# One stage for sample attention and sample mixers, and five raw buffers between the projection passes

## What is computed

```python
h = RMSNorm(x) * (1 + scale1(c)) + shift1(c)
proj = h @ w_in                     # columns of the mixers A, B, C, D
A: softmax attention over the own chunk of 64 and the 8 chunks before, with a relative bias
B: mLSTM: num = inter * (q @ c_state) + wqk @ v;  c = decay * c + (ws k)^T v;  n likewise
C: Mamba-2 SSD: y = (cb * dec * dt) @ x + exp(cs) * (C @ h_state);  h = exp(cs_end) * h + (wl x)^T B
D: gMLP spatial gating over chunks of 128
x = x + gate1(c) * (concat(A, B, C, D) @ w_out)
h2 = RMSNorm(x) * (1 + scale2(c)) + shift2(c)
x = x + gate2(c) * ((silu(causal_dwconv3(h2 @ w_gate)) * (h2 @ w_up)) @ w_down)
```

## Time and profile before

| | us |
|---|---|
| median of 3 runs | 3292.2 |
| the runs | 3286.8 to 3297.0 |
| profiled execution | 3301.0 |
| its span | 3299.0 |
| modulation and start | 0 to 147.2 |
| token pass | 147.2 to 514.7 |
| between the passes | 514.7 to 536.7 |
| channel pass | 536.7 to 831 |
| change of stage | 831 to 853.7 |
| sample attention | 853.7 to 970.5 |
| sample mixers | 970.5 to 1084.4 |
| mixers | 1084.4 to 1653 |
| feed forward | 1653 to 3299 |

### The profile page before, as it was taken

The page is one execution under the profiler, slowest core; times in us unless marked ns, Lnnn a source line. Parts: engine busy times, 40 slices in busy tenths (PEclk is TensorE's granted clock), DMA queues, the critical chain, the costliest instruction groups (busy, mean ns, idle before and its releaser), DMA issues.

```text
span 3299.0 us, 41922 instructions
## 1 busy us (share of the span) xinstructions
PE 2921.4 (89%) x16186; PEld 2581.5 (78%) x16186; DVE 1330.0 (40%) x2523; ACT 986.1 (30%) x1680; POOL 236.7 (7%) x405
## 2 busy tenths in 40 slices
PE   4599997999366399999779999999999999999987
PEld 1388886999233278888679999879999978999975
DVE  2333324332125355545333333544333454544444
ACT  1133324332111135445322222432222333222333
POOL 0000000000000133333100000000000000000000
PEclk8699998999775699999889999999999999999998
DMA  9522214221511653433152222443222354322344
GB/s 301 189 90 90 99 63 136 86 78 60 130 35 10 190 162 119 141 126 118 61 131 64 64 64 85 151 154 111 67 64 63 105 162 122 116 76 70 95 129 141
DMA packets 338040, 356.26 MB, mean 108 GB/s; under 512 B 44295, under 2 KB 279435, under 8 KB 337460
## 3 DMA queue, kind: packets, MB, share of 16 engines
q1 hardware_dynamic: 329238, 352.34, 34.6%
q10 hardware_dynamic: 8672, 2.15, 0.4%
HBM read 286.56 MB, written 70.10 MB: 108 GB/s over the span
## 4 chain that ended last, share of the span: by engine, by line
PE 44%; DMA 2%; DVE 2%; SPq 1%; issue 1%; ACT 0%; POOL 0%; DVEq 0%
PE acc_ps L2734 13%; PE acc_ps L2690 10%; PE acc_ps L2691 10%; PE acc_ps L2692 10%; DMA w_raw<-in_f_w_down 1%; DVE w_lo L2879 0%; DMA xr<-scratch_x 0%; SPq L2640 0%; DVE y L2951 0%; ACT w_hi L2783 0%; DMA out_y_prompt<-y 0%; DVE xr L2945 0%; DMA ffn_gate_in<-scratch_ffn_gate 0%; DVE prod L2939 0%; DVE mid_lo L2929 0%
## 5 line engine op out<-in xcount | busy, mean ns | idle before, releaser
L2690 PE MATMUL acc_ps<-h_hi,w_hi 128*128 128x384 f32 (+1 forms) x2112 | 690.4, 327 | 7.2 <-DVE w_lo L2879 7.1
L2691 PE MATMUL acc_ps<-h_lo,w_hi 128*128 128x384 f32 (+1 forms) x2112 | 689.7, 327 | 0.0
L2692 PE MATMUL acc_ps<-h_hi,w_lo 128*128 128x384 f32 (+1 forms) x2112 | 689.6, 327 | 0.0
L2879 DVE TENSOR_TENSOR w_lo<-w_raw,w_hi 128x1024 fp32r<-128x1024 f32 x264 | 323.4, 1225 | 695.3 <-ACT w_hi L2783 684.7
L2783 ACT ACTIVATE w_hi<-w_raw 128x1024 fp32r<-128x1024 f32 x264 | 279.8, 1060 | 845.7 <-PE acc_ps L2692 524.2
L2690 PEld LDWEIGHTS acc_ps<-h_hi,w_hi 128*128 128x128 f32 x2112 | 398.0, 188 | 8.2 <-DVE w_lo L2879 7.5
L2691 PEld LDWEIGHTS acc_ps<-h_lo,w_hi 128*128 128x128 f32 x2112 | 398.0, 188 | 0.1
L2692 PEld LDWEIGHTS acc_ps<-h_hi,w_lo 128*128 128x128 f32 x2112 | 397.9, 188 | 0.0
L2734 PE MATMUL acc_ps<-w_hi,mid_hi 128*128 128x512 f32 x748 | 237.8, 400 | 33.0 <-DVE mid_lo L2929 32.9
L2734 PE MATMUL acc_ps<-w_hi,mid_lo 128*128 128x512 f32 x748 | 234.3, 395 | 0.0
L2734 PE MATMUL acc_ps<-w_lo,mid_hi 128*128 128x512 f32 x748 | 234.0, 394 | 0.0
(11 more groups left out here) (481 smaller groups left out, 4182.2 us busy)
## 6 DMA issues: line engine op xcount, KB each, us to landing
w_raw<-in_f_w_down SPq DMA_DIRECT2D x132, 512.0 KB, 3.5
w_raw<-in_f_w_gate SPq DMA_DIRECT2D x66, 512.0 KB, 3.9
w_raw<-in_f_w_up SPq DMA_DIRECT2D x66, 512.0 KB, 3.9
w_ada<-in_w_ada SPq DMA_DIRECT2D x12, 2048.0 KB
m_bc<-scratch_bc SPq DMA_DIRECT2D x16, 768.0 KB, 5.1
scratch_tok<-p_m SPq DMA_DIRECT2D x17, 640.0 KB, 2.9
m_tok<-scratch_tok SPq DMA_DIRECT2D x16, 640.0 KB, 4.7
scratch_ht<-p_m SPq DMA_DIRECT2D x17, 512.0 KB, 3.3
```

What stands on the lines that cost most here:

```text
L2690: t.matmul(dst, hi, h2_hi[:, k, cols], start=(k == 0), stop=False)
L2691: t.matmul(dst, hi, h2_lo[:, k, cols], start=False, stop=False)
L2692: last = t.matmul(dst, lo, h2_hi[:, k, cols], start=False, stop=(k == KD - 1))
L2879: v.tensor_tensor(w_lo[j][:], raw[j][:], w_hi[j][:], ALU.subtract).then_inc(s_lo[j], 1)
```

## The change

**Between the projection passes.** The raw buffers of the channel weights become five. Buffer 3 lies in `rows`, which the token pass uses for its input, buffer 4 in the last third of `ht_in`, which group 0 (two tiles of the three) leaves free; it is loaded in pieces of 128 columns. In the turn of the last tile, SP issues `load_w(3)`, `load_w(4)` and `load_ht(0)` ahead of `store_rows(15)`; pieces 5 to 15 wait for the piece five before. `spatial` of the last tile moves behind unit 1 of group 0.

**The sample stage.** `sample_attention` and `sample_mixers` become `sample_stage` (L1200 of the new file). Two streams share a tile of 128 rows (2 streams x 4 heads x 16 tokens), so there are four rounds. `q_blk` holds block-diagonal queries: 32 columns (two heads of one stream) against 128 rows. The scores of a round are four products 32x512 on four column groups of the array and four of 16 columns for the new keys; the output is ten products of 256 columns, alternating between two halves of the columns. The old states are read per stream: 32 products of 65x16 (`old_c`) and 32 of 64x16 (`old_h`), which are turned afterwards; the masks and folds go. Weighings and the decay of the states move from DVE to POOL. C's state is turned by 16 transposes of 128x128 and isn't turned back, since the decayed state is kept as it was loaded. SP's queue carries keys, values and C's state (24 loads; a partition's share of keys is 4 KB in one piece); 29 smaller loads stand on ACT's queue ahead of its first operation. SP stores in the order y, m, ya (two for a round), n and c of B, and C's state in eight.

**The last down pass.** It is written out without a loop and has four raw buffers: two more in free columns of `mid` (`raw_far`), in eight pieces of 128 columns. Load f waits for the low part of f - 4.

The core of the diff:

```diff
@@ projections
-                if m >= 3:
-                    sp.wait_ge(s_wlo, m - 2)
+                if m >= NRAW:
+                    sp.wait_ge(s_wlo, m - NRAW + 1)
+                elif m >= 3:
+                    sp.wait_ge(s_t, NTT)
...
+                if n == LASTN:
+                    load_w(3)
+                    load_w(4)
+                    load_ht(0)
                 if n >= 1:
                     store_rows(n - 1)
...
-            load_ht(0)
-            for m in range(3, 2 * KD):
+            for m in range(NRAW, 2 * KD):
                 load_w(m)
...
-                spatial(n)
...
                     chan_unit(g, u)
+                    if g == 0 and u == 1:
+                        spatial(LASTN)
@@ sample_stage, PE
+            def scores(j):
...
+                for b2 in range(2):
+                    for pair in range(2):
+                        b, at = 2 * j + b2, (2 * b2 + pair) * 32
+                        w = q_blk[:, b, pair].rearrange("p r t -> p (r t)")
+                        t.matmul(m[at:at + 32, B_S, :], w, k_t[:, pair, b, :], start=True, stop=True)
...
+            def attend(j):
...
+                for n in range(NPAST + 1):
+                    for b2 in range(2):
+                        b, rows = 2 * j + b2, slice(b2 * DH, (b2 + 1) * DH)
+                        if n < NPAST:
+                            t.matmul(o_ps[rows], prob_t[:, n, rows], v_in[:, b, n, :], start=(n == 0), stop=False)
+                        else:
+                            last = t.matmul(o_ps[rows], own_t[:, rows], v_new[:, b, :], start=False, stop=True)
...
+            def old_h():
...
+                for b in range(NB):
+                    for h in range(H):
+                        at = h // 2 * P + b * TS
+                        last = t.matmul(m[half(h), B_E, at:at + TS], hst[:, b // 2, h, b % 2 * DH:(b % 2 + 1) * DH],
+                                        xc[:, 4 + h // 2, b * TS:(b + 1) * TS], start=True, stop=True)
...
+            turn_k(0)
+            turn_k(1)
...
+            scores(0)
+            turn_ssm()
+            old_c()
+            turn_probs(0)
+            old_h()
+            turn_k(2)
+            turn_k(3)
+            attend(0)
+            turn_old()
+            scores(1)
+            rows_to_all()
+            turn_probs(1)
...
@@ sample_stage, DVE: a round's output
+                v.tensor_tensor(pick_o[:], o_ps.rearrange(heads, h=H), spread(head_inv[:], 2, DH), ALU.mult
+                                ).then_inc(E["out_masked"], 1)
+                dve.wait_ge(E["out_masked"], j + 1)
+                v.tensor_reduce(ya[:, j, :], pick_o[:].rearrange("p h d -> p d h"), AX, ALU.add).then_inc(E["ya_done"], 1)
@@ feed_forward
+        raw_far = [mid[:, 4 + KD * j:4 + KD * (j + 1), last_width:last_width + P] for j in range(2)]
...
+            def load_dn_last(f):
+                j, base = f % 2, down_unit(LAST, 1, 0)
+                sp.wait_ge(s_lo[j], base + max(0, f // 2 - 1))
+                if f % 4 < 2:
+                    sp.dma_start(raw[j][:], wd[f]).then_inc(s_raw[j], 16)
+                else:
+                    sp.dma_start(raw_far[j], wd[f].rearrange("p (k c) -> p k c", k=KD)).then_inc(s_far[j], 16)
```

More of the change, by code:

```diff
@@ L264, in projections @@
         raw = sb("raw", [P, 3 * XW])
-        w_raw = [raw[:, j * XW:(j + 1) * XW] for j in range(3)]
+        w_raw = [raw[:, j * XW:(j + 1) * XW].rearrange("p (n c) -> p n c", c=P) for j in range(3)]
+        w_raw += [rows[:, 3 * D:3 * D + XW].rearrange("p (n c) -> p n c", c=P), ht_in[:, 0:KX, 2 * P:TW]]
         ws_in = raw[:, 0:512].rearrange("p (g s) -> p g s", g=H)
@@ new lines, in new_c @@
+            def new_c():
+                for h in range(H):
+                    pe.wait_ge(E["vws_done"], h + 1)
+                    if h == 2:
+                        pe.wait_ge(E["dec_args"], 1)
+                    for q in range(2):
+                        last = t.matmul(m[half(h), (B_T, B_X)[h // 2] + q, 0:4 * W1], tok[:, T_KB + h * DH:T_KB + (h + 1) * DH],
+                                        vws[h % 2][:, 4 * q * W1:(4 * q + 4) * W1], start=True, stop=True)
+                    last.then_inc(E["c_ps"], 1)
@@ L1724, in mixers @@
+            add_c(2)
+            add_c(3)
+            extract(3)
+            for h in range(H):
+                add_h(h)
 def mixers(nc, sem, A, O, S, c, keep, par):
@@ L2657, in _ @@
                 for a in range(NPASS):
+                    if s == LAST and a == 1:
+                        for f in range(KF):
+                            load_dn_last(f)
+                            if f >= 3 and f - 3 < len(before(s, a)):
+                                store(before(s, a)[f - 3])
+                        continue
                     lo, hi = static_until(s, a)
@@ L2841, in _ @@
                 for a in range(NPASS):
+                    if s == LAST and a == 1:
+                        for f in range(KF):
+                            down_step_last(f)
+                            tile_part(f, before(s, a))
+                        continue
                     lo, hi = static_until(s, a)
```

801 lines of the change are left out of this document (437 added, 364 removed).

## The result

The changed kernel takes 3170.5 us as the median of four runs (3166.2 to 3176.7), the kernel before 3292.4 beside it. The ratio is 0.9622, with a 95% interval of 0.9604 to 0.9639: 124 us less by the ratio, 122 by the two medians. The forecast was 3179, in a range of 3153 to 3215. The profiled execution has a span of 3166.4 us.

The account below looks back on a forecast made before the run. TensorE is busy most of the span, so the prediction took its idle stretches, between projection passes and in the chained sample blocks, as the places to gain: 91 + 20 + 2 = 113 us off 3292.2, hence 3179, range 3153 to 3215.

Parts of the forecast that it names:

- The passes: Between the projections' token and channel passes: early loads remove PE's idle time, 20 us saved, bounds 8.6 and 22.
- The sample stage: One stage replacing sample attention and sample mixers: 140 us instead of 230.7, 91 us saved.
- The head: Start of the sample stage: ACT issues 29 loads before its first operation, 0.89 us each, hence 26 us.
- Rival E: Start of the sample stage: ACT's issues hold it, 59 or 88 us more, 3238 or 3267 us; chance 0.04.
- The list: PE's remaining products in the sample stage: 103 us at low clock, 59 at full, 82 at clock 0.66.
- The waits: Score rounds in the sample stage waiting on other engines: 8 us at low clock, 17 at full, 11 taken.
- The tail: End of the sample stage: stores of y_s' rows, states and ssm still end it, 22 us.
- The last down pass: Steps 6 to 19 with four raw buffers: load leaves the buffer's cycle, 2 us saved, between 0 and 4.
- B: Sample stage runs at 1.2 GHz throughout: 159 us, total saving 94, kernel 3198 us; chance 0.24.
- C: Sample stage reaches 2.4 GHz: 124 us, total saving 129, kernel 3163 us; chance 0.18.
- A: The forecast itself, whole kernel: 91 + 20 + 2 = 113 us saved, 3179 us; chance 0.50.
- D: Gap between the projection passes closes by the h^T wait alone: 91 + 9 + 2, 3190 us; chance 0.04.

## Why the prediction was right, step by step

**The passes: 20 us forecast.** Measured 19.7 in the trace (the first unit at 516.98 instead of 536.73) and 22.8 by time, with an interval (18 to 28) that holds 20. The walk through ACT's list put the first unit at about 516, with about 1 us of idle left and the last two pieces behind the token pass's end, and the trace shows all three.

**The sample stage: 91 us forecast, 98 measured.** The sum was 26 of head, 93 of list and waits, 22 of tail: 140.7, which the prediction put at 140. The trace has 39.0, then 70.3 until the last round's output at 943.2, then 23.5: 132.8. So two terms were wrong in opposite directions, by 13 and 23 us, and that the sum came out within 8 us is partly luck.

- *The head.* The step that priced all 29 issues at 0.89 us failed. The 21 small ones cost less, 0.5, and the eight of B's state 3.5 on average. Rival E named the mechanism and I gave it 0.04, with a single price for all issues; it came for 8 of 29, and the average over all, 39.0/29 = 1.34, stayed below the 1.5 from which the forecast said it would be wrong. What I had not weighed is that SP issues 9 MB at the same time. The rows that I took the price from stood beside less than 3 MB of loads.
- *The list.* It was forecast at 82 us, at a clock of 0.66. Behind the head PE had this list done in 60 us of busy time, at a granted clock of 0.83:

```profile
877.25:946.50 69.25, 59.97 (x486) 43.90 (x486) 32.69 (x110) 23.20 (x48) 19.30 (x22) 0.83 0.03 7
```

  So both factors were wrong, in the same direction. The stage's mean clock of 0.68 looks like a hit, but it holds the head, 39 us at 0.50 with PE all but idle, and the tail. The 0.66 was the mean of the two old blocks and was put on the list alone; their busy parts (860 to 970.5 and 997 to 1060 us) had run at 0.80 and 0.50, and the new list ran faster than either. With 0.83 the prediction's own formula gives 59 + 44 × (1/0.83 − 1) = 68 us, 14 less. The other 8 are prices, nearly all of one kind: the 64 old-state products were put at 20.5 and 12.8 us at the two levels, some 14.4 at this clock, and took 6.9. I had taken the 0.43 us of a small product with 128 columns of weights down to 0.32 for 64 columns; grouped, such a product costs 0.18 at the lower clock, and alternating between column halves 0.11. Smaller slips changed little: half of ten products of 256 columns is 4.85 us and not 4.65 at the lower clock. The 16 instructions of the key transposes are 16 transposes, as the prediction counted them, and not eight, as the start of this text says of transposes. A round's scores took 1.29 us at the higher level, where 1.46 was forecast, a round's output 2.6, as forecast, and C's new state 4.2, where 4.3 was.
- *The waits.* In the body PE was not busy for 13.2 us; 11 had been taken. DVE stayed below PE, as forecast (29.9 against 53.3 us busy). POOL's scalings took 1.0 us and its weighings 1.0 to 1.3, 1.2 forecast, but they were not all hidden: 3.25 us of PE's waiting is for one of them.
- *The tail.* 23.5 us, 22 forecast, and for a reason that the sum did not have: it took the old tail over whole, and the old tail, too, had the stores of n in it. The 9.00 us of ya's eight stores are no price of theirs: an issue took 0.50 to 0.59 us, and SP waited 4.5 us among them for the last round's output.

**The last down pass: 2 us forecast.** Steps 6 to 19 run from 3100.83 to 3142.2, 2.96 us each instead of 3.06, 1.4 us in all; the first of them:

```profile
3100.83 0.73 PE L2873 MATMUL acc_ps<-w_hi,mid_hi 128*128 128x512 f32 x2 [2.72 <-DVE mid_lo L3099]
```

Another 1.7 us lie behind step 20 (from there to the end 21.8 us instead of 23.5). By time 3.6 us, between 1 and 7.

**The rivals.** B (the lower clock throughout, 3198) and C (the higher throughout, 3163) both missed the clock, which changed between the levels. The measured 3170.5 lies between A and C because the clock of the list was higher than A had it and the old-state products were cheaper, less the head's 13 us. D did not happen. E came in part, as said above. The rule of the Trainium skill that stands behind C ("TensorE: Matmul & The Clock Gate", Part 1) holds here only in part: the denser list ran at 0.83, where the busy parts of the old blocks had 0.80 and 0.50, but PE was busy without a gap from 891.3 to 894.7, and the granted clock of that window is 0.50.

The Trainium skill ("TensorE: Matmul & The Clock Gate", Part 3) says that a weight load overlaps products in flight only if the row group differs. C's old states all use the whole of the rows, and alternating column halves gave 56 ns an instruction instead of 91. Whether the loads or the products overlapped there no run shows, so this neither bears the sentence out nor refutes it; for the price of such products the measurement decides.

The Trainium skill ("DMA: Bandwidth & Descriptors", Rules for kernel authors) says that transfers of two partition halves should be one of 128 partitions. No run here stored the new stage's state of C that way. The eight half stores took 16.9 us from first issue to the next stage, where the one large store of before took 16.2, and 8.6 us once the stores of n were gone.

## What to carry to other kernels

A load that an engine issues ahead of its work belongs to that engine's critical path, and its price is not that of the nearest quiet row: beside bulk traffic an issue of 512 small pieces took up to 6 us. Put such loads on the queue of an engine that has nothing behind them, and ask of each state or row how many pieces its layout makes; 8 KB as 2048 single elements cost 8 us behind 1.5 MB of states. When a sum comes out right, compare its terms one by one: here 13 us too little and 23 too much left an error of 8, and each of the two pointed at something to gain or to learn. And don't put the mean clock of a stage on its busy part: the mean of 0.68 held a head at 0.50 in which PE all but stood idle, and the list ran at 0.83.

## What the runs showed of the hardware

- Eight DMAs of 512 pieces each took 27.9 us to issue on ACT's queue while SP issued 9 MB (0.65 us each for the first two, up to 6.05 for the others), and 9.5 us (0.61 to 2.31 each) when 7 MB of these waited.
- Stores of 2048 elements of 4 bytes lengthen the tail behind C's first store from 8.6 to 16.9 us, at a full DMA share and 78 GB/s.
- Products with 64 or 65 columns of weights and 16 moving columns: 52 ns an instruction in groups at the higher clock, 91 at the lower, and 56 at the lower if neighbours use different column halves.
- The changed kernel's stage took 132.8 and 140.1 us in two executions, by how soon and for how long the clock was at its higher level behind the head. The untouched mixers took 561 to 562 or 566 to 569 us in 14 traces, by whether the granted clock of the window 80 to 100 us into them was 1.00 or 0.74 to 0.83.
